# Transposed feed-forward up-projections, and two edits in the first attention projection

## The reference

```python
def swiglu(h, w_gate, w_up, w_down):                       # ffn0 to ffn3
    return (jax.nn.silu(h @ w_gate) * (h @ w_up)) @ w_down  # 1024 -> 2816 -> 1024

def conv_ffn(h, w_up, cw, cb, w_down):                     # ffn4 and ffn5
    gu = causal_dwconv(h @ w_up, cw, cb)                    # 3 taps over the tokens
    g, u = jnp.split(gu, 2, axis=-1)
    return (jax.nn.gelu(g, approximate=True) * u) @ w_down
```

## Time and profile before

| | us |
|---|---|
| median of 3 runs (2079.17 to 2114.07) | 2080.18 |
| the profiled execution | 2090.13 |
| its span | 2088.2 |
| PE busy | 1924.6 (92%) |
| DVE busy | 1458.5 (70%) |
| ACT busy | 943.3 (45%) |
| POOL busy | 308.1 (15%) |

### The profile page before, as it was taken

How to read it: one execution, slowest core, us unless ns; L and a number is a source line. 1 busy time by engine, 2 the same in 40 slices (tenths; PEclk the granted TensorE clock), 3 DMA queues, 4 the chain that set the end, 5 groups by cost and what they waited for, 6 DMA issues and landing times.

```text
span 2088.2 us, 26790 instructions
## 1 busy us (share of the span) xinstructions
PE 1924.6 (92%) x9206; PEld 1593.7 (76%) x9206; DVE 1458.5 (70%) x2119; ACT 943.3 (45%) x1320; POOL 308.1 (15%) x292
## 2 busy tenths in 40 slices
PE   3999889899999998999999899989889997979998
PEld 2888668678878886788889788877767786767786
DVE  7776778577777776667745555556569966656995
ACT  2444345444435443455544344444554445554443
POOL 0101011000110010000000000009612203931210
PEclk9999989899999999899989799999899999879999
DMA  7878565358886785354510455552154453124443
GB/s 308 302 278 295 181 224 202 104 201 280 277 286 252 279 292 193 126 185 174 181 67 1 139 181 181 192 183 98 61 184 172 170 182 141 62 81 150 172 164 118
DMA packets 61404, 381.99 MB, mean 183 GB/s; under 512 B 6896, under 2 KB 6896, under 8 KB 24448
## 3 DMA queue, kind: packets, MB, share of 16 engines
q1 hardware_dynamic: 41040, 300.96, 40.3%
q0 software_dynamic: 19856, 77.93, 11.2%
q10 hardware_dynamic: 432, 2.08, 0.2%
HBM read 379.89 MB, written 1.05 MB: 182 GB/s over the span
## 4 chain that ended last, share of the span: by engine, by line
PE 73%; DVE 14%; DMA 7%; issue 3%; ACT 2%; DVEq 0%; POOLq 0%; SPq 0%; ACTq 0%
PE ps L445 20%; PE ps L446 19%; PE ps L447 19%; DMA arena<-in_mod 7%; DVE ring_lo L1424 4%; PE ps L741 2%; DVE wc L1488 1%; PE ps L481 1%; PE ps L765 1%; PE ps L855 1%; PE ps L751 1%; DVE wb L1624 1%; PE ps L539 1%; PE ps L506 1%; PE ps L533 1%
## 5 line engine op out<-in xcount | busy, mean ns | idle before, releaser
L1424 DVE TENSOR_TENSOR ring_lo<-ring,w_hi 128x1024 fp32r<-128x1024 f32 x534 | 692.7, 1312 | 321.7 <-ACT w_hi L1037 319.8
L1037 ACT ACTIVATE w_hi<-ring 128x1024 fp32r<-128x1024 f32 x556 | 583.0, 1059 | 577.5 <-PE ps L447 566.5
L445 PE MATMUL ps<-w_hi,h_lo 128*128 128x512 f32 x1696 | 688.2, 406 | 43.8 <-DVE ring_lo L1424 11.4
L446 PE MATMUL ps<-ring_lo,h_hi 128*128 128x512 f32 x1696 | 673.8, 397 | 0.0
L447 PE MATMUL ps<-w_hi,h_hi 128*128 128x512 f32 x1696 | 673.6, 397 | 0.0
L445 PEld LDWEIGHTS ps<-w_hi,h_lo 128*128 128x128 f32 x1696 | 327.3, 193 | 123.3 <-DVE ring_lo L1424 17.9
L447 PEld LDWEIGHTS ps<-w_hi,h_hi 128*128 128x128 f32 x1696 | 326.2, 192 | 71.0
L446 PEld LDWEIGHTS ps<-ring_lo,h_hi 128*128 128x128 f32 x1696 | 327.1, 193 | 65.2
L445 PE MATMUL ps<-w_hi,hid_lo 128*128 128x512 f32 x528 | 209.2, 396 | 12.1 <-DVE ring_lo L1424 12.1
L446 PE MATMUL ps<-ring_lo,hid_hi 128*128 128x512 f32 x528 | 207.3, 393 | 0.0
L447 PE MATMUL ps<-w_hi,hid_hi 128*128 128x512 f32 x528 | 207.2, 392 | 0.0
(11 more groups left out here) (286 smaller groups left out, 1709.6 us busy)
## 6 DMA issues: line engine op xcount, KB each, us to landing
ring<-in_stream SPq DMA_DIRECT2D x278, 1024.0 KB, 4.8
arena<-in_mod POOLq DMA_DIRECT2D x128, 512.0 KB, 5.8
arena<-in_mod SPq DMA_DIRECT2D x3, 2048.0 KB, 17.1
gate<-in_wide POOLq DMA_DIRECT2D x3, 1536.0 KB, 11.1
arena<-in_nsaw POOLq DMA_DIRECT2D x2, 1072.0 KB, 10.5
arena<-in_mod SPq DMA_DIRECT2D x1, 1536.0 KB, 26.4
arena<-in_konst POOLq DMA_DIRECT2D x1, 1295.5 KB, 6.1
arena<-in_mixw POOLq DMA_DIRECT2D x2, 576.0 KB, 11.8
```

Of the source, the lines that this page charges most:

```text
L445: nc.tensor.matmul(dst, x_lo, hi, start=first(i), stop=False)
L446: nc.tensor.matmul(dst, x_hi, lo, start=False, stop=False)
L1037: nc.scalar.activation(w_hi[:, q % SPLITS, :], ring[:, half % SLOTS, (q % 2) * QUARTER:(q % 2 + 1) * QUARTER], ACT.Copy).then_inc(w_hi_rea ...
L1424: v.tensor_tensor(ring_lo[:, slot, cs], ring[:, slot, cs], w_hi[:, q % SPLITS, :], ALU.subtract).then_inc(w_lo_ready, 1)
```

## The change

The up-projection of all six feed-forward blocks swaps its operands: a chunk of 128 weight columns is stationary and the 256 tokens move. A quarter is then 24 matmuls of 256 columns, each with its own weight load, and the result has features on the partitions already. `turn_hidden` goes. The gate chunks fill the first bank of a step and the up chunks the second. `hid_hi` and `hid_lo` are made from `wb`, which now has two halves used in turns. In ffn4 and ffn5 ACT's copy goes too, and the convolution reads the projection's own banks, in two halves (gate chunks, then up chunks) with a split between them; PE's next use of the banks waits for `fconv_ready`. In the first attention ACT copies the q/k banks to `wb` first and frees them with that, then squares and norms from `wb`; the copy of transposed q/k comes before the exponentials; the forget sums move from after quarter 5 to after quarter 7 on PE, and from place 6 to place 8 on DVE.

```diff
+            def up_turned(q, bank, it, per, fresh):
+                for r in range(4):
+                    if fresh is not None:
+                        pe.wait_ge(fresh[0], fresh[1] + r + 1)
+                    low_part(q + r, it, per)          # waits for ring_lo, as quarter did
+                    slot, half, buf = ((q + r) // 2) % SLOTS, ((q + r) % 2) * QUARTER, (q + r) % SPLITS
+                    for i in range(2):
+                        for b in range(4):
+                            o = i * 512 + b * P
+                            hi, lo = w_hi[:, buf, o:o + P], ring_lo[:, slot, half + o:half + o + P]
+                            x_hi, x_lo = h_hi[:, 2 * r + i, :], h_lo[:, 2 * r + i, :]
+                            dst = ps[:, bank + b // 2, (b % 2) * T:(b % 2 + 1) * T]
+                            nc.tensor.matmul(dst, hi, x_lo, start=(r == 0 and i == 0 and b % 2 == 0), stop=False)
+                            nc.tensor.matmul(dst, hi, x_hi, start=False, stop=False)
+                            mm = nc.tensor.matmul(dst, lo, x_hi, start=False, stop=(r == 3 and i == 1 and b % 2 == 1))
+                    mm.then_inc(quarter_done, 1)
...
                 def step(j, it):                       # PE, all six blocks
-                        pe.wait_ge(gu_ready if conv else h_ready, val(it, v0 + j - RING + 1))
-                    up(q0 + 4 * j, UP_BANKS[j % 2], it, TURNQ, (norm_lo, 4 * m) if j == 0 else None)
-                    if j > 0:
-                        turn_hidden(j - 1, it)
+                        pe.wait_ge(fconv_ready if conv else h_ready, val(it, v0 + j - RING + 1))
+                    up_turned(q0 + 4 * j, UP_BANKS[j % 2], it, TURNQ, (norm_lo, 4 * m) if j == 0 else None)
...
+                pe.wait_ge(fconv_ready if conv else h_ready, v0 + UPS - 1)
+                for kk in range(DOWNQ):
+                    if kk % 2 == 0:
+                        pe.wait_ge(hid_ready_all, UPS * f + kk // 2 + 1)
...
-                    if n == 5:
+                    if n == 7:
                         running_sums()
...
                 def step(j, it):                       # ACT, ffn4 and ffn5
-                    split(q, q + 3, it, TURNQ)
-                    act.wait_ge(quarter_done, val(it, q, TURNQ))
-                    act.wait_ge(tr_done, val(it, u))
-                    nc.scalar.activation(wa[:, :], psf[:, b * 512:(b + 2) * 512], ACT.Copy).then_inc(gu_ready, 1)
-                    split(q + 3, q + 4, it, TURNQ)
+                    split(q, q + 2, it, TURNQ)
                     if j > 0:
                         gelu(j - 1, it)
+                    split(q + 2, q + 4, it, TURNQ)
...
                 def squares(z):                        # ACT, first attention
-                    act.wait_ge(qk_read, z)
-                    nc.scalar.activation(wa[:, :], psf[:, b * 512:(b + 2) * 512], ACT.Square, scale=HD ** -0.5).then_inc(sq_ready, 1)
+                    act.wait_ge(qk_T, z)
+                    nc.scalar.activation(wb[:, :], psf[:, b * 512:(b + 2) * 512], ACT.Copy).then_inc(qk_read, 1)
+                    act.wait_ge(qk_read, z + 1)
+                    nc.scalar.activation(wa[:, :], wb[:, :], ACT.Square, scale=HD ** -0.5).then_inc(sq_ready, 1)
...
+                    if w in FOX_QK:                    # ACT, now ahead of exps
+                        keep_qk(FOX_QK[w])
                     if w in FOX_S:
                         exps(FOX_S[w])
-                    if w in FOX_QK:
-                        keep_qk(FOX_QK[w])
...
                 def step(j, it):                       # DVE, ffn4 and ffn5
                     q = q0 + 4 * j + 4
-                    split(q, q + 3, it, TURNQ)
+                    split(q, q + 1, it, TURNQ)
                     if j > 0:
-                        conv(j - 1, it)
-                    split(q + 3, q + 4, it, TURNQ)
+                        conv(j - 1, it, (0, 1))
+                    split(q + 1, q + 2, it, TURNQ)     # POOL's quarter: DVE skips it
+                    if j > 0:
+                        conv(j - 1, it, (2, 3))
+                    split(q + 2, q + 3, it, TURNQ)
                     if j > 0:
                         join(j - 1, it)
+                    split(q + 3, q + 4, it, TURNQ)
```

More of the change, by code:

```diff
@@ L428, in _, with low_part @@
         def _(pe):
-            def quarter(q, it, per, lhs, out_of, first, last, ends=False):
+            def low_part(q, it, per):
                 before = sum(p < q for p in POOL_Q)
@@ L437, in quarter @@
                     pe.wait_ge(w_lo_ready, val(it, q + 1 - before, per - mine))
+            def quarter(q, it, per, lhs, out_of, first, last, ends=False):
+                low_part(q, it, per)
                 slot, half, buf = (q // 2) % SLOTS, (q % 2) * QUARTER, q % SPLITS
@@ L1085, in keep_hi @@
             def keep_hi(f, j, it):
-                act.wait_ge(tr_done, val(it, UPS * f + j + 1))
-                o = val(it, j * 512, RING * 512)
-                nc.scalar.activation(hid_hi[:, bass.ds(o, 512)], ps[:, 6, :], ACT.Copy).then_inc(hid_hi_ready, 1)
+                act.wait_ge(h_ready, val(it, UPS * f + j + 1))
+                o, half = val(it, j * 512, RING * 512), (j % 2) * 512
+                nc.scalar.activation(hid_hi[:, bass.ds(o, 512)], wb[:, half:half + 512], ACT.Copy).then_inc(hid_hi_ready, 1)
             def ffn(f):
@@ L1098, in step @@
                     act.wait_ge(h_ready, val(it, u))
-                    nc.scalar.activation(wa[:, 0:512].rearrange("p (t n) -> p t n", t=NT), ps[:, b:b + 2, 0:C2],
-                                         ACT.Silu).then_inc(silu_ready, 1)
+                    nc.scalar.activation(wa[:, 0:512], ps[:, b, :], ACT.Silu).then_inc(silu_ready, 1)
                     if j > 0:
@@ L1132, in ffn_conv @@
                         step(PEEL + r, it)
-                turned = q0 + UPQ + DOWNQ // 2 - 1 + SPLITS
-                split(q0 + UPQ + 4, turned)
                 gelu(UPS - 1, None)
-                split(turned, q0 + UPQ + DOWNQ + LEAD)
+                split(q0 + UPQ + 4, q0 + UPQ + DOWNQ + LEAD)
             def qkv(q0, z0, w0, bufs, groups):
@@ L1555, in keep @@
                     dve.wait_ge(hid_hi_ready, val(it, UPS * f + j + 1, turn))
-                    o = val(it, j * 512, turn * 512)
-                    v.tensor_tensor(hid_lo[:, bass.ds(o, 512)], ps[:, 6, :], hid_hi[:, bass.ds(o, 512)], ALU.subtract).then_inc(tr_copied, 1)
+                    o, half = val(it, j * 512, turn * 512), (j % 2) * 512
+                    v.tensor_tensor(hid_lo[:, bass.ds(o, 512)], wb[:, half:half + 512], hid_hi[:, bass.ds(o, 512)], ALU.subtract).then_inc(hid_ready_all, 1)
                 def step(j, it):
@@ L1568, in step @@
                     dve.wait_ge(silu_ready, val(it, u + 1, turn))
-                    dve.wait_ge(tr_done, val(it, u, turn))
-                    v.tensor_tensor(wb[:, 0:512].rearrange("p (t n) -> p t n", t=NT), ps[:, b:b + 2, C2:512],
-                                    wa[:, 0:512].rearrange("p (t n) -> p t n", t=NT), ALU.mult).then_inc(h_ready, 1)
+                    half = (j % 2) * 512
+                    v.tensor_tensor(wb[:, half:half + 512], ps[:, b + 1, :], wa[:, 0:512], ALU.mult).then_inc(h_ready, 1)
                     if j > 0:
@@ L1660, in ffn_conv @@
                 d0 = q0 + UPQ
-                turned = d0 + DOWNQ // 2 - 1 + SPLITS
-                split(d0 + 4, turned)
-                conv(UPS - 1, None)
+                conv(UPS - 1, None, (0, 1))
+                conv(UPS - 1, None, (2, 3))
+                split(d0 + 4, d0 + 5)
                 join(UPS - 1, None)
-                split(turned, d0 + DOWNQ + LEAD)
+                split(d0 + 5, d0 + DOWNQ + LEAD)
             def angles():
@@ L1823, in fox @@
                         forget_log()
-                    if n == 6:
+                    if n == 8:
                         forget_sums()
```

68 lines of the change are left out of this document (23 added, 45 removed).

## The result

The changed kernel takes 2074.32 us (median of 20 runs, 2054.53 to 2105.68), the kernel before in the same comparison 2082.57 (20 runs): ratio 0.993, 95% interval 0.9901 to 0.9958. A program falls into a slower state in some executions: the ratio leaves these out, while the medians are of all executions and lie 8.25 us or 0.4% apart. By the ratio it is faster by 0.7%, where 1.6% was forecast. The measured 2074.32 is 28 us above the forecast 2046 and lies inside the range, near its upper end. Its profiled execution took 2076.79 us with a span of 2075.1, 13.1 shorter than the span before.

The account below looks back on a forecast made before the run. PE, busy 92% of the span, was taken as the bound, with DVE setting the step in ffn4 and ffn5. Gains of 4.7 + 24 + 5 = 34 us off 2090.13 gave 2056, less 9.95 for the median 2046; range 2026 to 2076.

Parts of the forecast that it names:

- PE's price per quarter: Up-projections: 24 matmuls of 256 columns at 0.117 us each, 2.81 a quarter; own range 0.115 to 0.120.
- The even point of 0.1182: Up-projections of ffn0 to ffn3: price in us per matmul at which 96 matmuls equal the old step of 11.35.
- the step from the profiled execution to the median: Whole kernel: median taken as 9.95 us below the profiled execution, turning 2056 into 2046.
- ffn0 to ffn3: Steps of these blocks fall from 11.35 to 11.25 us; 44 steps gain 4.7 us.
- ffn4 and ffn5: DVE's collision with POOL's split, 2.2 us a step, goes and PE sets the step at 11.25; 24 us gained.
- the new wait: ffn4 and ffn5: PE waits for the convolution of step j-2, ready at 10.1, wanted at 11.25; hidden.
- Rival 1: ffn4 and ffn5: POOL's split still shuts DVE out; -6 in place of +24 us, 2076; chance 0.12.
- First attention: Moved sums, ACT's early copy and the clock: sum 4.4, taken as 5 us gained, ends 0 and 12.
- The wait for the gain: First attention, PE's turn of the first q/k step: waits 1.9 us for DVE's gain in place of 4.9.
- The head outputs' wait: First attention, output projection: a third of the 5.5 us wait, 1.7, estimated as gained.
- my terms up to there: First attention: 2.6 us getting through DVE's queue, plus about 1.1 from ACT's copy ahead of the exponentials.
- Rival 2: Loads show before each 256-column up-projection matmul; gain gone at 0.1225 us, nothing covered 2750 us; chance 0.06.

Follow-up runs that it names:

- experiment 5: Changed kernel, up-projection matmuls cut to other column and load sizes in ffn0 to ffn3, work left out; 192 columns start 0.1117 us apart, 256 behind narrow loads 0.1133.
- experiment 4: Kernel before with only ffn0 to ffn3 transposed, no attention edits: 2090.86 us, ratio 1.0029.
- experiment 7: Kernel before with all splits on DVE, none on POOL, nothing transposed: 2074.87 us, ratio 0.9953.
- 2: Changed kernel with ffn0 to ffn3 put back to the old orientation and turns; ffn4, ffn5 transposed, attention edits kept: 2065.88 us, ratio 0.991.
- 3: Kernel before with only the first attention's edits, nothing transposed: 2078.68 us, ratio 0.9979.
- experiment 10: Kernel before with the first attention's edits and no split on POOL, nothing transposed: 2074.32 us, ratio 0.9856 from 4 runs.
- 8: Kernel before with only the forget sums moved in the first attention: 2084.38 us, ratio 0.9973.
- 9: Kernel before with only ACT's copy of the q/k banks and the new order of ACT's copies: 2085.34 us, ratio 0.9971.
- 6: Kernel before, old orientation, up-projection matmuls cut to other sizes, work left out; behind loads of 128, 384 columns start 0.1733 us apart, 256 columns 0.120.

## Why the prediction was off

**The step that failed is PE's price per quarter.** I took 0.117 from the forget logits as "the nearest row"; the matmuls had the right columns, but their loads had 16 columns where the new ones have 128. Measured is 0.1200, or 11.52 a step where the sum had 11.25. Over 66 steps that is 18 us, against 20.6 us missing between the forecast's 33.7 and the 13.1 of the spans. The right number was in the rows: the earlier trace rows gives 226.7 ns for 512 columns behind loads of 128, which is 213.3 at 2.4 GHz and 13.3 over; the same constant on 106.7 is 120.0. I took the row with the same columns moving and carried over its constant; with 256 columns the constant goes with the load's width (experiment 5), so the row with the same load was nearer. Not all of the row's 10.4 ns is explained by that, as experiment 5 has 6.7 for the same two widths. The even point of 0.1182 stood in the text, and the own range reached 0.120, but I put the likeliest on the side that pays.

**A second term failed, the step from the profiled execution to the median.** The sum took 9.95 us off for it, as the three runs before had it. After the change the profiled execution lay 2.47 above the median (2076.79 against 2074.32). That is another 7.5 us, and the whole miss by the median is 28 (2046 forecast, 2074.32 measured): 18 for the price, 7.5 for this, and under 3 that single executions can't resolve. One execution's place among the others is no property of the kernel.

**ffn0 to ffn3** follow from that: 96 x 0.1200 = 11.52 against 11.35, so 0.17 a step lost, +7.5 over 44 steps where -4.7 was forecast. The stages gave +8.7, experiment 4 +6.3 (2090.86 less 2084.57). "The removed turns are nearly all eaten" had the right form and the wrong sign. DVE stayed where it was (6.23), ACT too.

**ffn4 and ffn5**: the mechanism is shown. POOL's split beside the convolution costs DVE nothing that shows (the first half of it 0.99 + 1.65, the second, all beside the split, 0.99 + 1.64), DVE's step is 10.32 (10.2 forecast), the new wait is hidden, PE sets the step; experiment 7 shows by itself that the collision held the old step at 12.35 rather than 11.78. At 11.52 the working gives 111.1 - 103.7 = 7.4 for nine steps, and with 2.7 for the last two turns and 0.64 lost in each of the first two steps, 8.8 per block. The stages gave 6.5 and 9.2, and ffn4 at equal clock 8.8. Two thirds of a step's gain come from the collision alone, without the transposition (experiment 7); the prediction did not ask for that. Rival 1 is refuted.

**First attention**: -5 forecast, -6.7 in its stage, -4.8 to -5.0 in the three executions with the same edits and ffn0 not transposed (experiments 2, 3 and 10). In 3 and 10 the stage's mean granted clock is 0.90, in the changed kernel's profile 0.93. The wait for the gain is 1.9 as forecast, and the clock is back at 1.00. The head outputs' wait gave 1.3 of the estimated 1.7. The chain up to the turn of the probabilities gained more than half: from the first forget logit to that turn it took 307.02 - 260.07 = 46.95 before. The turn in the timeline before, then the first forget logit and the turn after:

```profile
307.02 1.54 PE L666 MATMUL ps<-konst,arena 128*128 128x128 f32 x6 [3.98 <-ACT arena L1194]
...
262.34 0.28 PE L599 MATMUL ps<-h_hi,wf_lo 128*16 128x256 f32 x1
...
304.51 1.69 PE L665 MATMUL ps<-konst,arena 128*128 128x128 f32 x6 [3.85 <-ACT arena L1198]
```

After, it is 42.17, 4.8 less, where my terms up to there gave 2.6 + 1.1 = 3.7. The sums' move brings it; the copy by itself isn't shown to bring anything (experiments 8 and 9). That the whole came to 5 is in part luck: its terms were halves and thirds taken by estimate.

**Rival 2** (loads show) named the right place, and its price of 0.1225 to 0.227 a matmul did not come. The Trainium skill, "TensorE: Matmul & The Clock Gate", section "Part 3: Packing small matmuls", would have each load shown here, as both use all 128 rows; experiment 5's 0.1117 with 192 columns and the 0.1200 with 256 refute it, since a load of 0.11 in the open behind 0.107 would be over 0.2 (estimated from experiment 5). At most the 6.7 ns by which 128-column loads cost more than narrow ones can be a load that shows. That a single row can't tell a load from a constant is why 5 and 6 were needed: only a second size does.

What stays open: 512 columns behind narrow loads at 0.230, 256 columns behind loads of 16 at 0.1133 in one place and 0.1171 in another, and whether experiment 10 is as good as 2.

## What to carry to other kernels

Before work is turned so that it takes more and smaller matmuls, write the price as columns plus a constant, and take the constant from matmuls whose loads have the same width: at 13.3 ns, 48 more a step cost 0.64 us, more than the 0.47 of four transpositions and less than the 0.90 of eight. Where a second engine helps with elementwise work on SBUF, look at what its help costs the first: here taking it away altogether was worth 0.5%. Keep a change block by block: turned where the vector engine set the step and left alone where TensorE did, it has the lowest median.

## What the runs showed of the hardware beside this

- In one execution, a block whose matmuls have 128 columns behind loads of 128 (ffn1 of experiment 5) ran at the lower of the two clock levels, 1.2 GHz, for all of its 210 us, though PE shows as busy for 210.00: a granted clock of 0.50, and 210/986 = 0.213 per matmul. The 192 columns of ffn0 kept 1.00 once they had it. The clock had fallen before the block (0.50 from 407.4 on, the block's first matmul started at 414.8), and came back at 642.9, after the 512-column matmuls of the down-projection had begun at 640.1. In the same execution it stayed at 0.50 for 85 us more, in the second attention, whose code is unchanged and whose stage took 31 us longer than before; in no other execution here was it low for over 21 us at a time. All this is one execution, and a long stretch at the lower level isn't tied to 128 columns in it. What holds the clock down, no run here shows. The stretch behind the block and the one in the second attention:

```profile
642.90:660.00 17.10, 17.10 (x77) 14.12 (x76) 13.05 (x15) 6.38 (x6) 2.11 (x4) 1.00 0.84 287
1144.70:1230.00 85.30, 83.65 (x324) 75.14 (x322) 25.85 (x78) 20.50 (x46) 0.00 (x0) 0.50 0.02 7
```

- In the turned up-projection a 256-column matmul costs 0.1133 behind a load of 64 or 16 columns and 0.1200 behind 128.
- At the lower clock level, matmuls of 128, 192 and 256 columns behind loads of 128 all start 0.213 apart (experiment 5; in the changed kernel three of 256 columns take 1193.81 - 1193.17 = 0.64 us): there, going below 256 columns saves nothing.
- The same first step of a block takes 11.58 or 14.28 us by the granted clock it falls on (1.00 or 0.79), so a stage's time from one execution can't settle a term of under 3 us unless its granted clock is read beside it.
